# A transformer stack in one kernel: each dense product as one float32 matmul in place of three rounded ones

## What is computed

```python
# layer 1
h = rmsnorm(x, g_mix_pre);  proj = h @ w_in            # dilated attention + gated delta rule
mix = concat([out_a, out_b]) @ w_out
x = x + rmsnorm(mix, g_mix_post)
h = rmsnorm(x, g_ffn_pre)
x = x + rmsnorm((silu(h @ w_gate) * (h @ w_up)) @ w_down, g_ffn_post)
# layer 2 (x and context, modulated by a condition): neighbourhood and differential attention,
#   output projection, feed-forward with a 3-tap convolution on the gate, hidden width 2816
# layer 3 (x): grouped-query attention and a Hyena filter, output projection, feed-forward
```

## Time and profile before

| | |
|---|---|
| three timed runs | 2447.79, 2448.26, 2449.73 us |
| median | 2448.26 us |
| the profiled execution, span from the first to the last instruction | 2447.7 us |
| its mean granted TensorE clock | 0.997 of full speed |
| matmul side of TensorE busy | 2394.9 us (98%), 14385 records |
| weight loads busy | 1959.5 us (80%) |
| VectorE, ScalarE, GpSimd busy | 1495.8, 958.7, 831.6 us |
| moved by DMA | 227.41 MB, 93 GB/s |

### The profile page before, as it was taken

How to read it: one execution, slowest core, us unless ns; L and a number is a source line. 1 busy time by engine, 2 the same in 40 slices (tenths; PEclk the granted TensorE clock), 3 DMA queues, 4 the chain that set the end, 5 groups by cost and what they waited for, 6 DMA issues and landing times.

```text
span 2447.7 us, 37094 instructions
## 1 busy us (share of the span) xinstructions
PE 2394.9 (98%) x14385; PEld 1959.5 (80%) x14385; DVE 1495.8 (61%) x2056; ACT 958.7 (39%) x1531; POOL 831.6 (34%) x454
## 2 busy tenths in 40 slices
PE   8999999999999999999999999999999999999999
PEld 6778877888886878866888888888887758788887
DVE  5765755547666976585466766644778586524242
ACT  4566644232224645356342222122266332423232
POOL 2533033544442222233223323223234313354443
PEclk9999999999999999999999999999999999999999
DMA  7212023445441110120224434323311111232322
GB/s 251 87 63 84 3 69 119 138 147 180 138 142 39 61 35 20 52 76 2 69 95 137 147 120 138 113 94 95 129 65 47 61 60 61 86 112 95 101 97 86
DMA packets 64662, 227.41 MB, mean 93 GB/s; under 512 B 7040, under 2 KB 9088, under 8 KB 63882
## 3 DMA queue, kind: packets, MB, share of 16 engines
q1 hardware_dynamic: 51160, 176.05, 21.5%
q10 hardware_dynamic: 13362, 49.40, 6.1%
HBM read 223.30 MB, written 2.12 MB: 92 GB/s over the span
## 4 chain that ended last, share of the span: by engine, by line
PE 84%; DVE 7%; issue 4%; ACT 3%; POOL 2%; DMA 0%; SPq 0%; DVEq 0%; POOLq 0%; ACTq 0%
PE ps L277 23%; PE ps L278 23%; PE ps L279 23%; PE ps L1064 2%; PE ps L1324 2%; POOL w_lo L3401 1%; PE ps L1286 1%; DVE rstd L963 1%; PE ps L1081 1%; PE ps L1094 1%; PE ps L1304 1%; PE ps L362 1%; PE ps L361 1%; PE ps L360 1%; PE ps L3173 1%
## 5 line engine op out<-in xcount | busy, mean ns | idle before, releaser
L3401 POOL TENSOR_TENSOR w_lo<-ring,w_hi 128x1024 fp32r<-128x1024 f32 x288 | 703.9, 2444 | 1167.2 <-ACT w_hi L270 664.6
L277 PE MATMUL ps<-act_hi,w_hi 128*128 128x512 f32 (+1 forms) x2280 | 844.0, 370 | 8.5 <-DVE act_lo_mixer L605 2.9
L279 PE MATMUL ps<-act_hi,w_lo 128*128 128x512 f32 (+1 forms) x2280 | 829.7, 364 | 0.0
L278 PE MATMUL ps<-act_lo_ffn,w_hi 128*128 128x512 f32 (+1 forms) x1408 | 513.6, 365 | 0.0
L277 PEld LDWEIGHTS ps<-act_hi,w_hi 128*128 128x128 f32 x2280 | 430.0, 189 | 95.3 <-issue 13.8
L279 PEld LDWEIGHTS ps<-act_hi,w_lo 128*128 128x128 f32 x2280 | 429.3, 188 | 72.0
L270 ACT CAST w_hi<-ring 128x1024 fp32r<-128x1024 f32 (+1 forms) x167 | 172.7, 1034 | 627.1 <-PE ps L279 569.3
L1715 ACT CAST w_hi<-ring 128x1024 fp32r<-128x1024 f32 (+1 forms) x132 | 137.5, 1044 | 456.9 <-PE ps L279 456.9
L278 PEld LDWEIGHTS ps<-act_lo_ffn,w_hi 128*128 128x128 f32 x1408 | 265.6, 189 | 41.0
L1604 DVE SCALAR_TENSOR_TENSOR ada_place<-ada_place 128x1024 f32<-128x1024 f32 x180 | 279.8, 1554 | 24.5 <-DMA ada_place<-in_w_ada 10.1
L277 PE MATMUL ps<-hidden_hi,w_hi 128*128 128x512 f32 (+1 forms) x704 | 256.5, 364 | 1.8 <-DVE hidden_lo L1801 1.5
(11 more groups left out here) (465 smaller groups left out, 3224.7 us busy)
## 6 DMA issues: line engine op xcount, KB each, us to landing
ring<-in_w_ffn SPq DMA_DIRECT2D x204, 512.0 KB, 3.3
ada_place<-in_w_ada ACTq DMA_DIRECT2D x90, 512.0 KB, 4.2
ring<-in_w_gdn SPq DMA_DIRECT2D x16, 512.0 KB, 3.3
ring<-in_w_hy SPq DMA_DIRECT2D x12, 512.0 KB, 3.3
ring<-in_w_dil_qk SPq DMA_DIRECT2D x8, 512.0 KB, 8.7
ring<-in_w_out SPq DMA_DIRECT2D x8, 512.0 KB, 3.2
ring<-in_w_diff_qk SPq DMA_DIRECT2D x8, 512.0 KB, 3.3
ring<-in_w_na_qk SPq DMA_DIRECT2D x8, 512.0 KB, 3.3
```

The lines of the kernel that those rows point to most:

```text
L277: pe.matmul(out, w[0], x[0], start=start, stop=False)
L278: pe.matmul(out, w[0], x[1], start=False, stop=False)
L279: return pe.matmul(out, w[1], x[0], start=False, stop=stop)
L3401: pool.tensor_tensor(k.w_lo[:, a % SPLITS, :], k.ring[:, a % SLOTS, :], k.w_hi[:, a % SPLITS, :].bitcast(F32), ALU.subtract).then_inc(k.lo ...
```

## The change

Each dense product becomes one float32 matmul that reads its weights from the ring and its activation as it is. `products`, `split_ahead`, `split_half`, GpSimd's lowering, `w_hi`, `w_lo` and all lower halves of activations are gone. The ring has 8 slots, and a slot is free when its unit's product is done. A feed-forward makes all 22 hidden tiles, then each output over 22 blocks; its down weights are packed without padding, so that one output's blocks begin in the middle of a unit. The hardware loops are written out. Modulation rows are loaded by SP, in order with the weights, four places deep. Fillers are 256 columns of float32. More blocks of the next matrix stand beside the last steps of attentions.

```diff
-SLOTS = 4
-SPLITS = 2
-CHUNKS = ((0, 6), (6, 8), (14, 8))
-FFN_UNITS = 2 * FT + DT * len(CHUNKS)
+SLOTS = 8
+TOGETHER = 2
+FFN_UNITS = 3 * FT
...
-def products(pe, out, w, x, start, stop):
-    pe.matmul(out, w[0], x[0], start=start, stop=False)
-    pe.matmul(out, w[0], x[1], start=False, stop=False)
-    return pe.matmul(out, w[1], x[0], start=False, stop=stop)
...
+def unit_products(k, pe, bank, u, x, blocks, widths, ready=None, at=(0, DT)):
+    if at[0] == 0:
+        k.slot_ready(pe, u)
     for b in range(at[0], min(at[1], blocks)):
...
         for n in widths:
-            last = products(pe, k.bank(bank, n, col), w, (hi[:, b, col:col + n], lo[:, b, col:col + n]),
-                            b == 0, b == blocks - 1)
+            last = pe.matmul(k.bank(bank, n, col), k.weights(u, b), x[:, b, col:col + n], start=b == 0, stop=b == blocks - 1)
...
 def wide_products(k, pe, times, bank=7):
     for _ in range(times):
-        pe.matmul(k.bank(bank), k.h_hi[:, 0, 0:P], k.h_hi[:, 0, 0:S], start=True, stop=True)
+        pe.matmul(k.bank(bank, CTX), k.h[:, 0, 0:P], k.h[:, 0, 0:CTX], start=True, stop=True)
...
 def modulate_vector(k, v, name, layer, shift0, n):
...
-            dst, src, rstd = bufs[t % 3][:, a:b], k.x[:, t, a:b], norm_rstd(k, v, name, q)
+            dst, src, rstd = k.h[:, t, a:b], k.x[:, t, a:b], norm_rstd(k, v, name, q)
...
-        if t >= 1:
-            lower(t - 1)
-    lower(DT - 1)
...
 def ffn_tensor(f, pe, begin):
...
+    begin(pe)
+    for m in range(1, FT):
+        if m >= 2:
+            pe.wait_ge(f.hidden, f.tiles + m - 1)
+        for s in range(2):
+            unit_products(k, pe, 4 * (m % 2) + 2 * s, f.u0 + 2 * m + s, k.h, DT, widths)
+    for j in range(DT - 2 if f.norm in BOUNDARIES else DT):
...
+        for c in range(FT):
+            i = FT * j + c
+            u = f.u0 + 2 * FT + i // DT
...
+            for a, b in f.parts:
+                last = pe.matmul(k.ps[:, 1024 * (j % 3) + a:1024 * (j % 3) + b], k.weights(u, i % DT), f.hid(c)[:, a:b],
+                                 start=c == 0, stop=c == FT - 1)
...
+def load_row(k, sp, n):
+    places = 2 if n < ADA_FIRST else ROW_PLACES
+    if n >= places:
+        sp.wait_ge(k.ada_used, n - places + 1)
+    sp.dma_start(row_place(k, n), k.dram[f"w_ada{n // ADA}"][n % ADA]).then_inc(k.ada_landed[n % ROW_PLACES], 16)
...
 def sync_program(k, sp):
...
+            if u >= SLOTS:
+                sp.wait_ge(k.unit_done, u - SLOTS + 1)
...
+            sp.dma_start(k.ring[:, u % SLOTS, :], d[name][a]).then_inc(k.slot_landed[u % SLOTS], 16)
...
+            for row in rows[u]:
+                load_row(k, sp, row)
...
-NA_BESIDE, HY_BESIDE, MIX_E_BESIDE = (1, 1, 1, 0), (2, 2, 2, 0), (1, 1, 1, 0)
+NA_BESIDE, HY_BESIDE, MIX_E_BESIDE = (2, 2, 2, 0), (2, 2, 2, 0), (2, 2, 2, 0)
```

More of the change, by code:

```diff
@@ L107 @@
 BEGUN = ["w_dil_qk", "w_out1", "w_ffn1", "w_diff_qk", "w_out_e", "w_ffn2", "w_gqa", "w_out_o", "w_ffn3"]
-HALVED = {FIRST[name] + SPLITS: n for n, name in enumerate(BEGUN)}
+ROW_PLACES = 4
 class Serial:
     def __init__(self, eng, own):
[L116 to L125, removed]
+        self.eng, self.own, self.n = eng, own, 0
 def link(e, ins):
@@ L132, in link @@
     ins.then_inc(e.own, 1)
-    e.eng.wait_ge(e.own, e.n if e.at is None else e.at * e.per + (e.n - e.per))
+    e.eng.wait_ge(e.own, e.n)
 class Core:
@@ L235, in after, with slot_ready, weights @@
         eng.wait_ge(self.scalar_stages, STAGES.index(stage) + 1)
-    def slot_ready(self, eng, u, loop=None):
-        more = 0 if loop is None else loop[0] * (16 * loop[1] // SLOTS)
-        eng.wait_ge(self.slot_landed[u % SLOTS], more + 16 * (u // SLOTS + 1))
+    def slot_ready(self, eng, u):
+        eng.wait_ge(self.slot_landed[u % SLOTS], 16 * (u // SLOTS + 1))
+    def weights(self, u, b):
+        return self.ring[:, u % SLOTS, b * P:(b + 1) * P]
 def stage_end(k, eng, sem, stage, wait=True):
@@ L387, with made @@
 NORMS = ["norm1", "mix1_post", "norm2", "ffn1_post", "mod_a0", "mod_f0", "mod_f0_late", "mod_a1", "mod_a1_late", "mod_f1"]
-LOWERED = ["input", "norm1", "norm2", "mod_a0", "mod_f0", "mod_f0_late", "mod_a1", "mod_a1_late", "mod_f1"]
+MADE = ["input", "norm1", "norm2", "mod_a0", "mod_f0", "mod_f0_late", "mod_a1", "mod_a1_late", "mod_f1"]
+SCALED = ["mod_a0", "mod_f0", "mod_f0_late", "mod_a1", "mod_a1_late", "mod_f1"]
+def made(k, name):
+    return lambda b: [(k.sem("norm_made"), DT * MADE.index(name) + b + 1)]
 def norms_before(name):
@@ L1568, in per_loop, with out_ready @@
[L1568 to L1587 removed]
+    def out_ready(self, j):
+        ends, rest = divmod(FT * (j + 1), DT)
+        return (self.out_made, self.made + j + 1 - (j + 1) // 4) if rest else (self.k.unit_done, self.u0 + 2 * FT + ends)
@@ L1769, in ffn_scalar @@
+    for j in range(DT - 2 if f.norm in BOUNDARIES else DT):
+        if f.norm is not None:
+            s.eng.wait_ge(f.added, f.outs + j + 1)
+            norm_square(k, s, f.norm, j, k.x if f.total is None else f.total, n, k.probs)
+            if j == DT - 1:
+                norm_root(k, s, f.norm, n)
     if f.norm in BOUNDARIES:
@@ new lines, in ffn_vector @@
+    if f.ada == 1:
+        f.ada_bias(v, 0, ADA_LATE, ADA)
+    if f.layer is None:
+        context_gather_vector(k, v)
+    for j in range(DT - 2 if f.norm in BOUNDARIES else DT):
+        buf = 1024 * (j % 3)
+        if f.layer is None and j == 5:
+            context_keep_vector(k, v)
+        if f.norm is not None and j >= 2:
+            norm_gather(k, v, f.norm, j - 1, n, k.probs)
+        v.eng.wait_ge(*f.out_ready(j))
+        if f.layer is None:
+            ins = v.eng.tensor_copy(f.total[:, j, :], k.bank(2 * (j % 3)))
+        else:
+            for q, (a, b) in enumerate(f.parts):
+                ins = v.eng.scalar_tensor_tensor(k.x[:, j, a:b], k.ps[:, buf + a:buf + b],
+                                                 k.mod[:, f.layer, 40 + j, q:q + 1], k.x[:, j, a:b],
+                                                 ALU.mult, ALU.add)
+                if q < len(f.parts) - 1:
+                    link(v, ins)
+        ins.then_inc(f.added, 1)
+        v.eng.wait_ge(f.added, f.outs + j + 1)
+        if f.norm is not None and j == DT - 1:
+            norm_invert(k, v, f.norm, n)
+        for row in f.rows[FT + j]:
+            f.ada_tile(v, row)
@@ L2994, in gdn_scan_scalar @@
     scaled(PAIRS - 1)
-    for h in range(GH):
-        s.eng.wait_ge(k.sem("gdn_out_normed"), h + 1)
-        mix_split_scalar(k, s, "mix1", S, (4 + h,))
-    split_half(k, s, "w_out1")
 def gdn_scan_vector(k, v):
```

854 lines of the change are left out of this document (240 added, 614 removed).

## The result

The changed kernel takes 2906.14 us (median of 4 runs, 2905.74 to 2907.63), the kernel before 2448.14 in the same comparison. The ratio is 1.187, with a 95% interval of 1.1853 to 1.1887. The forecast was 2891 with a range of 2855 to 2925: right in sign, within the range, 15 us low. The profiled execution took 2907.63 us; its span is 2905.7, with a mean granted clock of 0.999.

The account below looks back on a forecast made before the run. The prediction took TensorE's matmuls to bound the kernel, 69% of the chain being the three terms of a dense product. 2447.7 + 475 - 34 + 8 - 6 = 2890.7 us of span, 2891 timed, range 2855 to 2925.

Parts of the forecast that it names:

- The price of a product: Dense products on TensorE: 512 columns from 0.677 to 0.858 us, pairs from 1.047 to 1.290; +475 us in all.
- The counts: Dense products: 2376 of 512 columns and 736 of 256, unaltered by the change, with two records each after it.
- What goes with the splits: Stalls of TensorE at ten hand-overs and small gaps at feed-forward borders go: -34 us, bounds 10 and 53.
- Fillers: 95 wide_products fillers go from 0.226 to 0.432 us; many sit just before waits: +8 us of at most 20.
- Attention: ScalarE and VectorE lose splits beside the neighbourhood attention, whose matmuls wait 8.0 us for copies: -6 us, bounds 0 and -8.
- Weights and rows: Ring units held until their product is done, and modulation rows on SP's queue: both costed at nothing.
- 1 (more comes back): All of TensorE's idle time gone gives 2870 us; chance 0.06 of ending under 2855.
- its second part: Dense records of before at 0.230 us apart, not 0.226, outside steady stretches: 29 us more, giving 2841.
- 2 (a new wait; a falling clock): SP's queue delivers weights late, 3036 us, chance 0.05; or granted clock falls, 24 us per 1% at half speed, chance 0.04.
- 3: A dense float32 product is one record of 0.429 us: about 1711 us; chance 0.03.
- 4: Operands still read as rounded ones, with one pass: 628 us of dense work; chance 0.01.
- One reading: From POOL's waits of 664.6 and 502.6 us and ScalarE's of 569.3 and 456.9: splits are early and wait for TensorE.

Follow-up runs that it names:

- e1: Kernel before, each dense product one float32 matmul of the two upper halves, all splits still made: 2903.94 us, ratio 1.1863.
- e6: Kernel before, in the first two units after a norm or mix TensorE waits for the lower half only before the third term: 2447.34 us, ratio 0.9993.
- e3: Changed kernel with fillers of 128 float32 columns in place of 256: 2888.35 us, 17.8 less than the changed kernel.
- e4: Kernel before with fillers of 256 rounded columns in place of 512: 2450.57 us, ratio 1.0006.
- e7: Changed kernel with six ring slots in place of eight: 2913.31 us, 7.2 more than the changed kernel.
- e2: Kernel before with only the upper x upper term of each dense product, all splits still made: 2041.31 us, ratio 0.8338.
- e5: Kernel before with only the upper x upper term and no work for the lower halves, semaphores still counted: 1688.45 us, ratio 0.6893.

## Why the prediction was right, and where its 15 us are

**The price of a product** was the argument, and it held by every number. Forecast 0.858 us for 512 columns and 1.290 for a pair; measured 0.855 and 1.286 in the windows, 0.858 and 1.290 by the medians. It could be read ahead of the change because line 3173 ran the same operation in the same kernel. That this price is the cause is shown by e1. The two statements of the Trainium skill that the prediction weighed stand as it put them. Its "FP8 and Floating Point Precision", section TensorE Precision Notes, with four passes for true FP32, fits the changed kernel nearly: 0.858 us is 3.8 times the 0.226 of one rounded matmul. The halved rate of the Trainium skill's "Perfetto Trace Analysis", section Engine Utilization, fits one record (0.429 us, 1.9 times 0.226), and a product has two.

**The counts** held: 2376 and 736 products, twice as many records, one of them missing in the trace.

**What goes with the splits**, -34 us, came out at -32 with the two corrections below the table (-33 without). The amount is right, the reason only in part. In e1 all splits are still made, and yet only about 8 of these 32 us are missing (3 of dense time, 5 of waits). The other 24 come with the slower product itself: TensorE now takes so long over a tile that nothing is late for it, whether lower halves are made or not. Nor was it all stalls, as the prediction has it: TensorE's idle time next to dense products fell from 12.9 to 0.2 us. The rest was in records that started up to some 0.1 us late without an idle gap to be seen, in stretches with 0.236 us from start to start, and in time at the lower clock level (17 us before, 7 after). How these divide was not settled, and that they add up so near to 34 is in part luck. mod_a0 goes as foretold. Changed kernel, there:

```profile
912.92 2.74 PE L347 MATMUL ps<-consts 128*128 128x512 f32 x6
915.63 9.70 PE L257 MATMUL ps<-act,ring 128*128 128x512 f32 x29
```

```profile
912.77 11.38 DVE L547 SCALAR_TENSOR_TENSOR act<-x_res,mod,ps 128x512 f32<-128x512 f32 x16 [1.80 <-PE ps L407]
```

VectorE makes the eight tiles in 11.38 us, 1.42 each, in place of 2.61, and TensorE no longer waits once its keep_warm ends. e6 adds a correction: the late first product cost nothing of its own while VectorE's pace set the end. And e1, at 2.58 us of TensorE a tile against VectorE's 2.6, lost nothing but its first 1.54 us.

**Fillers**, +8: mis-sized. They cost 12.8 by the table, 14 with the wait behind keep_warm put right, and 17.8 came back when they were made as long as before in time (e3). The prediction's reason, that they stand just before waits, is borne out for the rounded fillers (e4: shortening them gives nothing, but for at most 3.4 us that the clock took). The wrong inference was that one twice as long would be more than half hidden too. Most of what was added to them came out at the end.

**Attention**, -6: wrong. The other matmuls took 2.4 us more by the table and, with the corrections, as much as before. Their wait for ScalarE's copies fell only from 8.0 to 5.4 us:

```profile
PE ps L1231 <- ACT pair_turned L1259: 5.4, 11, 0.6
```

and this gain was lost again in pieces of about 1 us or less elsewhere. The misses are then 2 us (splits), 6 (fillers) and 6 (attention), of the 15.

**Weights and rows at nothing**: right with eight slots. No wait on the ring and none of TensorE on rows appears. Whether six would do was left open, and e7 shows that they would for weights, but not for the Hyena tables.

**The rivals.** 1 (more comes back) is ruled out by the time itself, 2906 where it has 2870; its second part, dense records of before that are slower outside the steady stretches, was partly true and is in the 32 us above. (Its 29 us count the pairs twice, whose 1.047 us already hold the 0.230; for the 1640 others it is 20 us. And of the 52.8 us idle, 10 lie before TensorE's first and behind its last record, where no change of price reaches.) 2 (a new wait; a falling clock) did not happen; the clock rose from 0.997 to 0.999. 3 and 4 fail on the record counts and on the time.

**One reading was too easy.** That ScalarE and GpSimd wait hundreds of microseconds for one another and for TensorE says that in these waits TensorE was in the end the one waited for; it does not say how far the others were ahead. e2 says: not far, since a third of the product made the first feed-forward only 17% quicker. The prediction needed only the sign, and so was not hurt.

## What to carry to other kernels

Before replacing several quick matmuls with one exact one, find the exact kind in the trace of the same kernel and take its pitch, from one start to the next, and the number of its records per matmul; here two records of 0.429 us stood against three of 0.226, and that one comparison with the counts gave +475 us where the kernel lost 458. Work on other engines that a busy TensorE hides is worth little when removed (about 8 us between e1 and the changed kernel), and a lot once the matmul work really shrinks (353 us between e2 and e5), so its size must be known before that step. Fillers and side loads are tuned to durations, and a late one costs its wait and then some clock (e7: 3.7 us and 3.4): when an instruction's price or a ring's length changes, they have to be fitted again (e3: 18 us, e7: 7 us).

## What the runs showed of the hardware that I had not expected

- With one term in place of three (e2) TensorE was busy 69% of the span and its mean granted clock was 0.846; in e5, busy 77%, 0.899; in the full kernels 0.997 and 0.999. In these runs short waits spread over the whole kernel went with the lower clock.
- Without GpSimd's subtractions beside it VectorE is faster at the same instruction: a modulation row took 1554 ns before and 2001 ns in e2, where the two engines overlap more, 1224 ns in the changed kernel (line 1468) and 1225 in e5, where the subtractions are gone. These means hide two values. Before, the 149 rows that started while GpSimd was idle took 1224 to 1228 ns each. Of the 31 that started while a GpSimd instruction ran, each ended 1079 to 1088 ns after that instruction's end. e2 has 71 such rows, which end 1080 to 1089 ns after. So here such a row stood nearly still until GpSimd's subtraction was done, and took up to 2.2 us longer. In neither full kernel did TensorE wait for these rows, so this was worth nothing.

```profile
L1468 DVE SCALAR_TENSOR_TENSOR ada_place<-mix,ada_place 128x1024 f32<-128x1024 f32 x180 | 220.3, 1224 | 5.8 <-DMA mix<-in_w_ada 1.1
```

```profile
L1600 DVE SCALAR_TENSOR_TENSOR ada_place<-ada_place 128x1024 f32<-128x1024 f32 x180 | 360.2, 2001 | 23.3 <-DMA ada_place<-in_w_ada 8.9
```
